# Causal scores from fp32r halves in place of f32 products, in a two-block kernel on one core

## The reference, cut to what matters

```python
def dilated_attention(q, k, v, positions, g_q, g_k):
    q = partial_rope(rms_norm(q, g_q), positions).astype(jnp.float32) * (ATTN_HEAD_DIM ** -0.5)
    k = partial_rope(rms_norm(k, g_k), positions).astype(jnp.float32)
    ...
s = jnp.einsum('bnqrhd,bnkrhd->bnrhqk', qb, kband)
...
p = jnp.exp(s - m)
```

## Time and profile before

| what | value |
|---|---|
| time, median of 3 runs | 3776.86 us (3775.34 to 3776.95) |
| time of the profiled execution | 3776.72 us |
| span in its trace | 3774.6 us |
| instructions | 53108 |
| PE busy | 3252.4 us, 86% |
| DVE busy | 2451.0 us, 65% |
| ACT busy | 1433.2 us, 38% |
| mean granted TensorE clock | 0.934 |

### The profile page before, as it was taken

The page is one execution under the profiler, slowest core; times in us unless marked ns, Lnnn a source line. Parts: engine busy times, 40 slices in busy tenths (PEclk is TensorE's granted clock), DMA queues, the critical chain, the costliest instruction groups (busy, mean ns, idle before and its releaser), DMA issues.

```text
span 3774.6 us, 53108 instructions
## 1 busy us (share of the span) xinstructions
PE 3252.4 (86%) x20990; PEld 2708.7 (72%) x20990; DVE 2451.0 (65%) x3251; ACT 1433.2 (38%) x2083; POOL 896.7 (24%) x624
## 2 busy tenths in 40 slices
PE   8998999999999999999999998866666676666678
PEld 8987888999999999999998998622222232222248
DVE  6568866554455556874646656877777776555566
ACT  6455656543354444664445454310100010100025
POOL 2000010000000100000000011465555565656622
PEclk9999999999999999999999999988888888787899
DMA  6433344565555565455553456999999999999974
GB/s 220 154 116 114 113 158 131 180 190 179 181 185 188 182 203 173 165 186 184 173 180 97 156 179 251 364 422 422 421 421 421 421 421 422 421 422 421 422 280 159
DMA packets 188023, 952.85 MB, mean 252 GB/s; under 512 B 20992, under 2 KB 21120, under 8 KB 121984
## 3 DMA queue, kind: packets, MB, share of 16 engines
q0 software_dynamic: 73728, 536.90, 34.4%
q1 hardware_dynamic: 114048, 412.56, 33.8%
HBM read 947.29 MB, written 2.10 MB: 252 GB/s over the span
## 4 chain that ended last, share of the span: by engine, by line
PE 59%; DMA 21%; DVE 10%; POOL 4%; ACT 3%; issue 2%; DVEq 0%; ACTq 0%; SPq 0%; POOLq 0%
PE ps L584 59%; DMA HLF<-in_peer_v,CS 8%; DMA BIG<-in_peer_v,CS 6%; DMA HLF<-in_peer_u,CS 3%; DVE HL L1882 2%; POOL BIG L566 2%; DMA HF<-in_peer_v,CS 2%; POOL HLF L566 2%; DVE BIG L1886 1%; DVE BIG L1882 1%; ACT HL L1209 1%; DMA BIG<-in_peer_u,CS 1%; ACT BIG L1203 1%; DVE BIG L1878 1%; DVE HLF L2564 0%
## 5 line engine op out<-in xcount | busy, mean ns | idle before, releaser
L584 PE MATMUL ps<-HS,HL 128*128 128x256 f32 x10128 | 1323.0, 285 | 8.3 <-DVE HS L1882 5.0
L584 PEld LDWEIGHTS ps<-HS,HL 128*128 128x128 f32 x10128 | 1270.8, 193 | 15.3 <-issue 8.1
L1882 DVE TENSOR_TENSOR HL<-RAW,HL 128x1024 fp32r<-128x1024 f32 (+1 forms) x772 | 949.7, 1230 | 281.1 <-ACT HL L1209 220.9
L1209 ACT CAST HL<-RAW 128x1024 fp32r<-128x1024 f32 (+1 forms) x772 | 805.5, 1043 | 538.9 <-PE ps L584 272.9
L584 PE MATMUL ps<-BIGR,HL 128*128 128x256 f32 x6720 | 897.1, 285 | 13.1 <-DVE HL L1882 10.9
L584 PEld LDWEIGHTS ps<-BIGR,HL 128*128 128x128 f32 x6720 | 852.6, 193 | 19.9 <-issue 14.8
L584 PE MATMUL ps<-HLF,HF 128*128 128x512 f32 x740 | 400.9, 697 | 220.3 <-DMA HLF<-in_peer_v,CS 204.4
L584 PEld LDWEIGHTS ps<-HLF,HF 128*128 128x128 f32 x740 | 161.0, 226 | 457.5 <-issue 396.8
L584 PE MATMUL ps<-BIG,HF 128*128 128x512 f32 (+2 forms) x656 | 333.8, 655 | 144.4 <-DMA BIG<-in_peer_v,CS 134.9
L2564 DVE CUSTOM_DVE_ANT_0 HLF<-HLF,BIG 128x2048 f32<-128x2048 f32 x120 | 275.1, 2293 | 181.9 <-DMA HLF<-in_peer_u,CS 176.4
L584 PEld LDWEIGHTS ps<-BIG,HF 128*128 128x128 f32 (+1 forms) x656 | 135.9, 218 | 336.3 <-issue 303.2
(11 more groups left out here) (205 smaller groups left out, 2163.3 us busy)
## 6 DMA issues: line engine op xcount, KB each, us to landing
RAW<-in_w_up SPq DMA_DIRECT2D x128, 512.0 KB, 3.8
RAW<-in_w_down SPq DMA_DIRECT2D x128, 512.0 KB, 4.3
RAW<-in_w_out SPq DMA_DIRECT2D x64, 512.0 KB, 3.4
RAW<-in_w_qk SPq DMA_DIRECT2D x32, 512.0 KB, 3.3
RAW<-in_w_xbc SPq DMA_DIRECT2D x32, 512.0 KB, 3.3
RAW<-in_w_xr SPq DMA_DIRECT2D x32, 512.0 KB, 3.6
RAW<-in_w_yr SPq DMA_DIRECT2D x32, 512.0 KB, 3.5
RAW<-in_w_gr SPq DMA_DIRECT2D x32, 512.0 KB, 4.1
```

The costliest lines, as they stand in the source:

```text
L584: return e.matmul(o, l, r, start=start, stop=stop, skip_group_check=True)
L1209: s.done(e.copy(o, i), sig)
L1882: v.done(e.tensor_tensor(o, a, b, op), sig)
```

## The change

QK is used as fp32r under the name QKH. ACT's copy of a turned bank now writes the rounded values and signals a semaphore of its own, s_qkhi. DVE then subtracts them from the bank and writes the rest to QKL, in room that the x/B/C chunks of w_xbc take later, and this subtraction, not the copy, frees the bank. PE makes three fp32r products in place of each f32 product. The two subtractions take the place of two empty steps on DVE, so that `prepared` still has six. The evacuation of w_xbc gets a wait for the scores at chunks 0 and 8, since it writes over QKL.

```diff
+        QKH = bigr(0, 16)
+        QKL = [bigr(o, 4).rearrange("p (a c) t -> p a c t", a=2) for o in (10240, 11264, 8192, 9216)]
...
                 def score(b):
                     pe.wait_ge(s_free3, TURN3["qk"] + 2 * (h // 4) + 2)
+                    ql, kl = QKL[h // 4][lo:lo + 64, 0, c % 2, :], QKL[h // 4][lo:lo + 64, 1, c % 2, :]
                     for i, (at, w) in enumerate(CAUSAL):
-                        p = mm(b[:, at:at + w], QK[lo:lo + 64, c, i * 128:i * 128 + 128], QK[lo:lo + 64, 8 + c, 0:w],
-                               True, True)
+                        q, t = QKH[lo:lo + 64, c, i * 128:i * 128 + 128], ql[:, i * 128:i * 128 + 128]
+                        mm(b[:, at:at + w], t, QKH[lo:lo + 64, 8 + c, 0:w], True, False)
+                        mm(b[:, at:at + w], q, kl[:, 0:w], False, False)
+                        p = mm(b[:, at:at + w], q, QKH[lo:lo + 64, 8 + c, 0:w], False, True)
...
                     s.wait_ge(s_turn3, t)
-                    copy(QK[:, 8 * a + 2 * G:8 * a + 2 * G + 2, :], PS[3][:, :].rearrange("p (c t) -> p c t", c=2),
-                         (s_free3, t))
+                    copy(QKH[:, 8 * a + 2 * G:8 * a + 2 * G + 2, :], PS[3][:, :].rearrange("p (c t) -> p c t", c=2),
+                         (s_qkhi, 2 * G + a + 1))
...
                 tt(h[:, :, :, 0:16], RP[0], RP[1], ALU.add, (s_qkr, G + 1))
                 yield
                 yield
-                yield
-                yield
+                for a in range(2):
+                    v.wait_ge(s_qkhi, 2 * G + a + 1)
+                    tt(QKL[G][:, a, :, :], PS[3][:, :].rearrange("p (c t) -> p c t", c=2),
+                       QKH[:, 8 * a + 2 * G:8 * a + 2 * G + 2, :].bitcast(F32), ALU.subtract,
+                       (s_free3, TURN3["qk"] + 2 * G + a + 1))
+                    yield
...
                 c = (n + 8) % 16
+                if n in (0, 8):
+                    v.wait_ge(s_score, SCORE["attn"] + n + 8)
```

More of the change, by code:

```diff
@@ L396, in build @@
         s_turn3, s_free3 = sem("turn3_filled"), sem("turn3_free")
+        s_qkhi = sem("qk_high")
         s_max, s_exp, s_prob = sem("row_max"), sem("row_exp"), sem("probs_ready")
```

## The result

The changed kernel takes 3780.62 us (median of 20 runs) against 3776.24 us before (20 runs): the ratio is 1.0013, with a 95% interval from 1.0007 to 1.0019, so it is 2.6 to 7.2 us slower. One of the changed kernel's 20 runs took 5918.24 us, at a mean clock of 0.900, and is left out of the ratio. The forecast was 3777.8 us within 3771.5 to 3784.0. The profiled execution took 3780.57 us with a span of 3778.8, 4.2 longer than before.

A forecast was written before the change was run, and what follows sets the result against it. The chain was taken to alternate through the attention between PE and DVE, ACT, POOL, then mostly DVE to 491 us, then PE. Products -2.2, first group +0.5, middle groups 0, fourth +2.8 made +1.1 on 3776.7: 3777.8 us, range 3771.5 to 3784.

The forecast's parts named there:

- The products, -2.2 us: PE's score steps: six fp32r products for two f32, 0.62 us a step, 0.23 less, over 9.6 steps on the chain.
- The signs that I named: Score step in the new profile: 0.62 us expected; near 0.75 weights' loads set the pace; over 1.2 narrow products aren't cheaper.
- the first rival: PE's score steps: narrow fp32r product no cheaper than f32, 0.32 us; +4.7 in place of -2.2, 3784.7 us; chance 0.13.
- Which steps lie on the chain: Of 16 score steps, six at full clock and two at half clock, 1.8 times as long, count: 9.6 steps.
- Passes of f32: Score products by the skill's four passes for FP32: 0.16 us saved a head, term -1.5, sum +1.8.
- First group, +0.5 us: First group's bank return: PE's second transposes wait for DVE's subtraction, about +0.5 us on the chain.
- Second and third, 0: Second and third groups' bank returns: DVE's waits of 2.71 and 4.11 us take up its lateness, 0.
- Fourth group, +2.8 us: Fourth group, DVE nearly full: waits and subtractions make 4.5 us, 1.72 of waiting absorbs part; +2.8, partly a new stall.
- Waits at chunks 0 and 8: Evacuation of w_xbc, waits for the scores at chunks 0 and 8: cost nothing, they aren't even written.
- The sum: Whole kernel: -2.2 + 0.5 + 0 + 0 + 2.8 = +1.1 us, 3777.8 us; chance 0.48.
- The second: Rival, fourth group: nothing of DVE's wait is taken up (+4.5), one more clock fall (+3); +5.8, 3782.5 us; chance 0.16.
- The third: Rival: subtractions are hidden, -2.2 + 0.5, 3775.0 us; with one clock fall less 3772.0; chance 0.18.

The follow-up runs named there:

- e1: Changed kernel without its hand-over: six fp32r products a head, all on rounded parts, no DVE subtractions, ACT's cast frees the bank; 3777.4 us, ratio 1.0001.
- e7: As e1, but a single fp32r product of the rounded parts for each block, two a head; 3772.01 us, ratio 0.9989 against the kernel before.
- e5: Changed kernel, with the first query block's three products over 256 columns in place of 128; single time 3781.92 us.
- e9: Changed kernel, with the first block's three products of 128 columns split into six of 64; single time 3787.26 us.
- e2: The f32 products of the kernel before with the changed kernel's hand-over: ACT copies in f32, DVE subtracts and frees the bank; 3780.6 us, ratio 1.0012.
- after_again: The changed kernel as it is, run and profiled a second time; 3779.25 us, ratio 1.001 against the kernel before.
- e3: Changed kernel, with DVE taking the next unit's low early, if next due, before each wait for ACT's cast; 3778.57 us, ratio 1.0009.
- e4: Changed kernel without the fourth group's subtractions: its heads use rounded parts in all products, the cast frees the bank; 3780.59 us, ratio 1.0008.
- e3_again: The same kernel as e3, compared once more with the kernel before; 3777.49 us, ratio 1.0005.

## Why the prediction was nearly right

**The products, -2.2 us.** This is the term that was mis-sized. I took 0.08 us for the narrow product from the transposes, as an fp32r product without a row of its own; the three take 0.39 us in place of 0.24 (0.17, 0.11 and 0.11), and the three wide ones 0.49 in place of 0.375 (0.17, 0.12 and 0.20), since the first of a width and the last before the dense products take longer. The step is 0.88 us in place of the 0.62 forecast, and 0.03 over the f32 one. The signs that I named were 0.62, 0.75 and 1.2 us; it is none of them. At half clock the step is 1.58 us in both kernels, so only the six at full clock count, and the term is +0.2. e1's 7.94 us in place of 7.90 from step to step say the same, and its time shows nothing within an interval from -3.0 to +3.8 us. The threshold that the first rival gave, 0.16 us a narrow product for nothing saved, lacked the wide ones' part of this. The rival's own 0.32 us did not come.

**Which steps lie on the chain.** I counted 9.6 from the chain of before, and overlooked a stretch of PE on it:

```profile
266.54 3.12 PE ps L584 x8
...
274.79 2.89 PE ps L584 x24
```

It holds the step at 268.01, at half clock, so before it is 11.4 steps. For the changed kernel this does no harm, since its hand-over takes the chain off PE there. By e7 the count is too high for larger gains: two of the four steps between 188 and 223 us are covered by ACT and DVE as soon as PE is 0.4 us faster. So with 0.62 us a step the term would probably have stayed short of -2.2 too; no run has such a step.

**Passes of f32.** The Trainium skill (FP8 and Floating Point Precision, TensorE Precision Notes) counts four passes for FP32. No run here tests the passes by themselves. The sum by it, +1.8, was nearer than mine, but not for its reason: it took the three products' columns for what they cost, and by e5 and e9 the columns of an fp32r product hardly count between 64 and 256.

**ACT's cast** takes 587 ns as the copy did: right. **DVE's subtraction** takes 692 ns, eight times: right.

**First group, +0.5 us**: 0.44 by the rows, 0.48 between e2 and the kernel before. Right. **Second and third, 0**: before the mask at 200.47 DVE waited only 0.28 us for PE in place of 2.71, and at 238.71 2.41 in place of 4.11; the cover was nearly used up in the second, as worked out, and held: e2 takes 35.13 us there against 35.14, and in the third group 41.43 against e1's 41.48. Right.

**Fourth group, +2.8 us**: 34.23 - 31.32 = 2.91; the stretch is 34.22 to 34.24 us in all five profiles that have the hand-over as it is (the changed kernel's, after_again, e2, e5, e9). The evacuation comes 2.91 us later counted from the stalled product before it (14.06 us after it, 11.15 before), as against 2.8. The new stall of 1.8 us at 285.5 is one of 1.74 that ends at 287.85. e3 and e4 take 2.51 and 2.62 of the 2.91 us away. Right, in the wait as in the size.

**Waits at chunks 0 and 8**: no wait shows there, and the first evacuation comes at 260.11 us behind its `low` as before. Right.

**The sum.** With the measured terms it is +0.4 in the first group, +0.2 in the steps up to the fourth, +2.9 there, and +0.3 from the last stall to 325 us, where the two traces are 3.85 us apart counted from the dense products at 156.6. That fits the intervals of both comparisons. The last 0.3 is the clock's and not the change's: the 24 dense products behind the half-clock step at 299 us take 4.19 us before, 4.51 in the changed kernel and 4.34 in after_again, and in e3 and e3_again, the same kernel twice, 5.49 and 4.44. In the profiled executions the distance went on to 5.8 us at the first cross-attention scores (591.90 against 586.12) and fell to 4.2 at the end. Behind 325 us no instruction differs; there the clock falls at other places: from 310 to 400 us its mean is 1.00 after and 0.96 before, from 495 to 590 us 0.96 and 1.00. So the traces are not a constant apart, as I had expected from w_z on, though the distance stays within the -3 to +7 that I gave. Which part of the last microsecond is the clock's can't be settled from single profiles.

**Luck.** The medians are 4.4 us apart, and I had forecast 1.1. The waits were right; the products' term was off by 2.4 us, in sign too, and that is most of the distance. The number lay in the range all the same, because the range was drawn for a fall of the clock, 3 us, and nearly for the first rival.

**Rivals.** The second, that nothing of DVE's wait is taken up, asked for 4.5 us in the fourth group: wrong, 2.9. The third, hidden subtractions, is what e3 makes nearly true. The further fall of the clock that the second feared came in after_again, behind the new stall, and cost the stretch nothing.

No version with the whole computation was faster than the kernel before. e3 is the best form of the change, and it gains nothing, because the six products don't save anything that could pay for the subtractions.

## What to carry to other kernels

Before f32 products are replaced by three fp32r ones, count products and not columns alone: in this kernel a product of 64 columns cost as much as one of 256, and a cheap price taken from a transpose did not hold for it. Where an engine must wait in its order for a neighbour's result, give it the next due piece of other work first; in this kernel one line took back 2.5 of 2.9 us. And where single runs differ by more than the effect, measure between two stalls that lie around the edit, and look at the clock between them.

## What the runs showed of the hardware that was not expected

An fp32r product of 64 rows costs 0.11 to 0.12 us at 64, 128 and 256 columns among its like (0.34 us for three more, 0.02 us for 384 more columns in all). The first product of a new width takes 0.14 to 0.22 us and the last before the dense ones 0.20 or 0.21 (0.17, 0.17 and 0.20 in the changed kernel; 0.22 and 0.21 in e5; 0.14, 0.21 and 0.21 in e9). A change of operands alone doesn't do it: each of the six products has its own, and in e5 the second block, of the same width, begins with 0.12. Six such products and two f32 products of the same shapes take the same 1.58 us at half clock, and 0.88 and 0.85 at full clock: both fall to about 0.55 of their speed. How long PE stays at half clock after a stall differs between executions of one kernel: 24 dense products at one place took 5.49 us in e3 and 4.44 in e3_again.
